# Two expert blocks before the overflow branch instead of one, and two buffers refilled in halves

## The reference

```
xs = h[row_tok]                      # tokens gathered by expert
def expert_block(xb, e):
    return (silu(xb @ w_gate[e]) * (xb @ w_up[e])) @ w_down[e]
y = zeros_like(h).at[row_tok].add(ys * row_w)   # each row scaled and added to its token
```

## Time and the profile before

| what | value |
|---|---|
| median of three runs | 1744.58 us |
| profiled execution | 1743.2 us, span 1741.4 us |
| TensorE matmul busy | 1624.5 us (93%) |
| VectorE busy | 653.8 us (38%) |
| read from HBM | 524.44 MB |
| mean granted TensorE clock | 0.973 |

### The profile page before, as it was taken

The page is one execution under the profiler, slowest core; times in us unless marked ns, Lnnn a source line. Parts: engine busy times, 40 slices in busy tenths (PEclk is TensorE's granted clock), DMA queues, the critical chain, the costliest instruction groups (busy, mean ns, idle before and its releaser), DMA issues.

```text
span 1741.4 us, 17712 instructions
## 1 busy us (share of the span) xinstructions
PE 1624.5 (93%) x6682; PEld 700.8 (40%) x6682; DVE 653.8 (38%) x1382; ACT 373.2 (21%) x919; POOL 71.2 (4%) x91
## 2 busy tenths in 40 slices
PE   5989998988999997998899999998889999979996
PEld 2435454462343332332344455444453333323332
DVE  2676665351323322323476122224531322322331
ACT  3023444231001010010410334333320101001000
POOL 1100000100000000000000000001000000000000
PEclk9999999999999998999999999998999999989999
DMA  9983823179999999999977021033389999999997
GB/s 353 372 308 100 288 97 146 52 285 389 430 426 426 425 428 427 427 428 419 364 240 243 1 97 49 1 124 123 141 365 420 427 423 427 429 426 426 428 427 293
DMA packets 109478, 526.64 MB, mean 302 GB/s; under 512 B 7921, under 2 KB 49122, under 8 KB 84682
## 3 DMA queue, kind: packets, MB, share of 16 engines
q1 hardware_dynamic: 80080, 486.56, 68.7%
q10 hardware_dynamic: 21322, 19.63, 3.6%
q0 software_dynamic: 7984, 19.22, 3.0%
HBM read 524.44 MB, written 8.48 MB: 306 GB/s over the span
## 4 chain that ended last, share of the span: by engine, by line
PE 81%; DMA 9%; DVE 5%; issue 2%; ACT 1%; SPq 1%; ACTq 0%; DVEq 0%
PE psum L2259 20%; PE psum L2290 11%; PE psum L2305 10%; PE psum L2016 10%; PE psum L1816 7%; PE psum L1988 4%; PE psum L1871 3%; DMA XN<-in_moe_w_up_dram 3%; DMA ring<-in_moe_w_up_dram 3%; DMA HT<-in_moe_w_down_dram 2%; PE psum L2237 2%; DVE W L1154 2%; DMA ring<-in_ada_w_dram 1%; PE psum L2123 1%; PE psum L1999 1%
## 5 line engine op out<-in xcount | busy, mean ns | idle before, releaser
L2259 PE MATMUL psum<-ring,V 128*32 128x512 f32 (+2 forms) x1376 | 352.3, 617 | 17.3 <-issue 9.4
L2305 PE MATMUL psum<-V,W 128*128 128x512 f32 x448 | 218.6, 613 | 3.6 <-DVE X L1606 1.1
L1606 DVE TENSOR_TENSOR X<-X,psum 128x512 f32<-128x512 f32 x224 | 153.7, 687 | 109.4 <-PE psum L2305 109.0
L2259 PEld LDWEIGHTS psum<-ring,V 128*32 128x32 f32 (+2 forms) x1376 | 115.9, 134 | 192.9 <-issue 192.6
L2290 PE MATMUL psum<-ring,V 128*64 128x512 f32 (+2 forms) x608 | 181.0, 596 | 0.8 <-issue 0.8
L1154 DVE SCALAR_TENSOR_TENSOR W<-ring,cact,W 128x512 f32<-128x512 f32 (+1 forms) x224 | 138.4, 618 | 7.7
L1046 ACT ACTIVATE V<-psum,modall,scls 128x128 f32<-128x128 f32 x216 | 81.2, 456 | 272.5 <-PE psum L2237 255.6
L2305 PEld LDWEIGHTS psum<-V,W 128*128 128x128 f32 x448 | 72.4, 188 | 148.5 <-DVE X L1606 85.3
L1055 ACT ACTIVATE V<-psum 128x512 f32<-128x512 f32 x28 | 16.7, 597 | 510.3 <-PE psum L2268 399.2
L2259 PE MATMUL psum<-HT,V 128*64 128x512 f32 (+2 forms) x224 | 102.4, 611 | 17.9 <-DMA XN<-in_moe_w_up_dram 17.5
L1816 PE MATMUL psum<-HT,ring 128*128 128x512 f32 x256 | 116.8, 602 | 0.0
(11 more groups left out here) (334 smaller groups left out, 1836.6 us busy)
## 6 DMA issues: line engine op xcount, KB each, us to landing
ring<-in_moe_w_up_dram SPq DMA_DIRECT2D x45, 2048.0 KB, 25.6
ring<-in_moe_w_gate_dram SPq DMA_DIRECT2D x41, 2048.0 KB, 25.3
ring<-in_moe_w_down_dram SPq DMA_DIRECT2D x38, 2048.0 KB, 25.4
ring<-in_ada_w_dram SPq DMA_DIRECT2D x16, 2048.0 KB, 15.8
HT<-in_moe_w_gate_dram SPq DMA_DIRECT2D x10, 2048.0 KB, 23.8
XN<-in_moe_w_up_dram SPq DMA_DIRECT2D x8, 2048.0 KB, 23.8
ring<-in_ada_w_dram ACTq DMA_DIRECT2D x16, 1024.0 KB, 5.2
T<-in_moe_w_up_dram SPq DMA_DIRECT2D x7, 2048.0 KB, 27.4
```

What stands on the lines that cost most here:

```text
L1606: return dve.tensor_tensor(x3[:, c, cols], x3[:, c, cols], sum_bank(p, hf, c), ALU.add)
L2259: ins = pe.matmul(bank[2 + 2 * i + b][half * w:(half + 1) * w, :], V[:, col:col + w], slot3(x)[:, k, :], start=(k == 0), stop=(k == KC - 1))
L2305: pe.matmul(sum_bank(p, hf, c), PICK[p % 2][:, c * P:(c + 1) * P], Y[:, hf * HALF:(hf + 1) * HALF], start=True, stop=True).then_inc(s["sum ...
```

## The change

It has two parts. First, `gate_up(1)` is taken out of `further_blocks()` and stands before the wait on `flag_ready`, the load of the flag and the branch. The order of TensorE's matmuls stays as it was. Second, loads 9 and 10, the first two that reuse a buffer (those of block 0's gates), are issued as two DMAs of 1 MB each. The first halves go out when TensorE has done four of the eight k-steps of block 0's gates (`first_gates`), since those four have used the first half of each buffer; the second halves go out when the gates are done, at which point load 9 went out before.

```diff
-DMAS = [2 if kind == "kq" else 1 for kind, _, _ in ORDER]
+REFILL = (len(HOMES[0]), len(HOMES[0]) + 1)
+DMAS = [2 if kind == "kq" or kind == "moe" and i in REFILL else 1 for kind, _, i in ORDER]
...
+        first_gates = sem("first_gates")
...
-                expert, ranked = {}, False
+                expert, ranked, refill = {}, False, {}
...
+                    if i in REFILL:
+                        sp.wait_ge(first_gates, l + 1)
+                        src = {"g": g, "u": u}[kind]
+                        sp.dma_start(slot(m + i)[:, 0:2 * D], src[:, 0:2 * D]).then_inc(w_in[SLOT[m + i]], 16)
+                        refill[i] = src
+                        if i == REFILL[1]:
+                            for x in REFILL:
+                                slot_free(m + x)
+                                sp.dma_start(slot(m + x)[:, 2 * D:4 * D], refill[x][:, 2 * D:4 * D]).then_inc(w_in[SLOT[m + x]], 16)
+                        continue
...
+                            if p == 0 and i == 0 and k == 3:
+                                ins.then_inc(first_gates, 1)
...
                 down(0)
 
+                gate_up(1)
+
                 def further_blocks():
 
-                    gate_up(1)
                     token_sums(0)
```

## The result

The changed kernel takes 1752.96 us, the median of five runs (1751.62 to 1753.43), against 1744.58 before (five runs, 1741.25 to 1746.43). The ratio is 1.005, with a 95% interval of 1.0039 to 1.0061: slower by 8.7 us, between 6.8 and 10.6. I had forecast 1750.6 in a range from 1740 to 1757. The profiled execution took 1752.78 us and its span is 1751.0, so 9.6 us more than before is to be found in it.

A forecast was written before the change was run, and what follows sets the result against it. TensorE and DMA are both near their limits; TensorE's lateness at block 5 less the slack delays each layer. +1.7 and +4.3 us make +6.0 on 1743.2, so 1749.2, plus 1.4 for the median: 1750.6, range 1740 to 1757.

The forecast's parts named there:

- the sum: Both layers' token-sum lateness, clock included, less slack: +1.7 us in layer 0, +4.3 in layer 1, together +6.0.
- the stall: TensorE idle at the moved branch, between block 1's ups and block 0's token sums: 5.9 us, bounds 4.5 and 7.4.
- the clock's cost: Half clock after idle time: 1.7 us at block 1's ups, 1.0 at the token sums, bounds 0 and 2.3 each.
- the gain of the refill: Loads 9 and 10 in halves put 2 MB in the queue earlier: 0.8 us in layer 0, 1.2 in layer 1.
- The slack: How late load 38 can go out at block 5 before the DMA stream breaks: 2.8 us, layer 1 3.0.
- The time behind the flag load: From TensorE's load of the flag to the first matmul behind the branch: 7.4 and 7.1 us.
- the cover: Matmuls queued ahead of the moved branch: about twelve of 0.11 us, hiding 1.3 us of its price.
- The lead of the stream: Transfers ahead before block 5, from refill and gate buffers freed sooner: 3.3 and 2.0 us.
- do not cancel: Rival that stall removed and stall added cancel, clock holding: total -1.7 us, 1742.9; chance 0.28.
- did not stay behind: Rival that the stall stays before block 1's gates and the moved branch is nearly free: -5.3 us, 1739.3; chance 0.07.
- the bounds: Rival with stall 7.4 us, clock 2.3 twice, refill gaining nothing: total +15, 1759.6; chance 0.10.

The follow-up runs named there:

- changed, again: The changed kernel, nothing altered, run once more for its profile; 1753.29 us.
- e1_branch_only: The changed kernel with loads 9 and 10 whole as before, only the branch moved behind block 1's ups; 1755.31 us, ratio 1.0058 to the kernel before.
- e2_refill_only: The changed kernel with the branch back in its old place, only the refill in halves kept; 1743.86 us, ratio 0.9999 to the kernel before.
- e3_branch_between: The changed kernel with the branch between block 1's gates and its ups, refill in halves; 1743.53 us, ratio 0.9991 to the kernel before.
- e4_no_branch: The changed kernel without TensorE's wait on the flag, its load and its branch; 1744.06 us, ratio 0.9997 to the kernel before.
- e5_delay3: The kernel before with three extra matmuls ahead of each layer's first token sums, no branch moved; 1748.50 us, ratio 1.0026 to the kernel before.
- e6_delay7: The kernel before with seven extra matmuls ahead of each layer's first token sums, no branch moved; 1755.13 us, ratio 1.0063 to the kernel before.
- e7_warm: The changed kernel with five extra matmuls between block 1's gates and ups, under the wait for load 13; 1749.02 us, ratio 1.0030 to the kernel before.
- e9_block9: The changed kernel with flag wait, flag load and branch moved between block 9's gates and ups; 1742.45 us, ratio 0.9993 to the kernel before.
- e10_block9_warm: e9_block9 plus five extra matmuls under the wait for load 13; 1743.44 us, ratio 0.9990 to the kernel before.
- e11_between_whole: e3_branch_between with loads 9 and 10 whole instead of in halves; 1744.01 us, ratio 0.9990 to the kernel before.

## Why the prediction was right

The mechanism was the one described, and the sum was 2.7 us too small (6.0 against 8.7). That it came so near is in part luck: the stall was shorter and the clock's cost a little larger than charged, the gain of the refill was missing in layer 0, and a term at the end of the program was not in the sum at all. Of the 9.6 us of the first profile only 4.2 lie in the two expert parts, of the 10.1 us of the second 8.7. The table gives, for both layers as layer 0 / layer 1, what each profiled execution has more than the one before, counted from block 0's gates: the issue of load 38, its landing, and the landing of the last down matrix (451.97 / 450.29 us before, from 391.51 to 843.48 and from 1276.69 to 1726.98).

| run | load 38 out | load 38 lands | last down lands |
|---|---|---|---|
| changed | 4.7 / 4.9 | 2.4 / 2.4 | 1.8 / 2.3 |
| changed, again | 7.7 / 6.1 | 5.5 / 3.7 | 4.9 / 3.8 |
| e1_branch_only | 4.0 / 8.5 | 1.8 / 6.1 | 1.1 / 6.0 |
| e2_refill_only | -0.1 / -1.2 | -0.3 / 0.4 | -0.4 / 0.6 |
| e3_branch_between | 0.0 / 2.1 | not recorded / -0.8 | -2.1 / -0.8 |
| e4_no_branch | -1.2 / -0.7 | -1.2 / -0.3 | -1.6 / -0.1 |
| e5_delay3 | 4.0 / 3.8 | 1.2 / 1.3 | 0.8 / 1.4 |
| e6_delay7 | 9.8 / 5.2 | 7.0 / 2.1 | 6.5 / 2.1 |
| e7_warm | 3.6 / 5.4 | 1.3 / 2.9 | 0.7 / 3.0 |
| e9_block9 | -1.8 / -0.8 | -2.0 / -0.3 | -2.4 / -0.3 |
| e10_block9_warm | -2.4 / -2.8 | not recorded / -1.5 | -2.3 / -1.6 |
| e11_between_whole | 0.8 / 1.6 | 0.4 / 0.0 | -0.7 / -0.4 |

*The slack.* In the six executions with a late TensorE, twelve cases, the first column less the second is 2.2 to 3.1 us, whether load 38 is 4 or 10 us late. (The lateness of load 38 stands here for that of TensorE, whose gates free its buffer.) I had taken 2.8 and 3.0; 2.3 and 2.5 hold for the changed kernel, as a lone load took 7.9 and 8.0 us and not 7.5. In layer 1 of e3_branch_between slack and lead together cover a lateness whole: load 38 goes out 2.1 us later than before and still lands sooner. The Trainium skill's fixed cost and rate (DMA: Bandwidth & Descriptors) gave an estimate of 6.8 us, and the traces do not agree: 7.4 to 8.1. That section is on DMAs that GpSimd issues, and these loads are SyncE's. In these twelve cases what is late at the landing of load 38 is late at the end of the part within 0.7 us. That the stream sets the time behind block 5, and TensorE up to it, is shown.

*The stall.* I had 5.9 us; it is 4.56 and 4.14. The time behind the flag load was right (7.3 and 6.9). The step that failed is the cover: "about twelve" matmuls queued ahead, 1.3 us. The ups end at 440.60 and 1327.98, 2.7 and 2.8 us behind the flag loads, which is some 24 matmul instructions of 0.11 us. What stayed nearly the same was the time that is covered, 2.5 us in the kernel before, and not the count. The stall moved with the branch in every run that shows it, and left with it. The rule of the Trainium skill's page Runtime: NRT & Kernel Launch (instruction fetch mechanics), that a taken branch waits for a fetch, fits this; no run shows that the stall is a fetch.

*The clock.* At the ups I charged 1.7 and it is 1.4 and 1.5 (8.44 on the chain of layer 0, and 8.53, for 7.07). At the token sums I charged 1.0 and it is 1.6 and 1.4 (9.58 and 9.38 for 7.97). In layer 0 of the second execution it is 2.4 at the ups and at least 2.1 at the token sums. These terms vary from one execution to the next more than anything else in the sum.

*The lead of the stream.* I had the stream 3.3 and 2.0 us ahead before block 5. Load 37, the last one issued before block 5's gates are done, lands 2.1 and 0.7 us sooner than before in the first profile, and no sooner in the second. In layer 0 the refill gives nothing: load 13 lands 38.1 us behind block 0's gates, 37.4 before. In layer 1 it lands 2.2 us sooner there (37.2 against 39.4), though other executions with the halves have up to 38.7. I had priced the refill by a dip in the GB/s, but the queue was not dry when load 9 went out before: load 8 landed 1.9 us later in layer 0 and 0.6 in layer 1. Both refills are in at 20.3 us behind block 0's gates in the changed kernel and 20.2 before in layer 0, at 20.0 and 21.4 in layer 1. The lead before block 5 is lost at block 5 in any case, but where load 13 lands sets when the ups start, and so the lateness. Because that lead is smaller than I thought, the expert parts of e3, e4 and e9 gain 1.7 to 2.9 us together and not 5.

*The sum.* Predicted +1.7 and +4.3; the first profile shows +1.8 and +2.3, the second +4.9 and +3.8. In the first, the token sums start 3.2 us late in layer 0, for which I had 3.5, and that agreement is luck: load 13 landed 1.4 us later than I put it, and the stall was 1.3 us shorter. In layer 1 they start 3.5 us late and not 6.3, since the stall was 1.8 us shorter and load 13 landed 1.0 us sooner than I put it.

*What I had no step for.* Behind the last landing of layer 1 the changed kernel takes 16.2 us to the end in both its profiles, 14.4 before. The chain after, then before (L2359 and L2344 are the last down products, L2319 and L2305 the last token sums):

```profile
1734.79 3.06 PE psum L2359 x16
1737.85 7.60 PE psum L2319 x16
```

```profile
1727.02 1.11 PE psum L2344 x8
...
1729.12 7.12 PE psum L2305 x16
```

The clock was granted at half there. It was in e1, e3, e4, e6, e9 and e11 too (15.8 to 16.2 us), and not in e2, e5, e7 and e10 (14.4 to 14.8). As e6 has neither part of the change, the fall does not need it; it gives back 1 to 2 us of what e3, e4 and e9 gained. Whether chance or the order of waits at the end decides it is open. Of the rest of the 9.6 us in the first profile, 2.5 lie before block 0 and 1.1 between the expert parts; the second execution has neither, and has its 10.1 us as -0.5, 4.9, 0.1, 3.8 and 1.8.

The rivals fall. The two parts do not cancel: the clock fell at both waits, and the median lies 10 us above that rival's. In layer 1 it was nearer than I allowed, though, for its token sums were to start 3.3 us late and start 3.5 us late in the first profile (4.7 in the second). The stall did not stay behind, since the gap behind the flag load is 7.3 and 6.9 us and not under 2. And the bounds were not all reached: 8.7 us and not 15.

## What to carry to other kernels

When a fixed order of buffers feeds an engine that is nearly as busy as the transfers, find the place where all buffers belong to the work at hand. The lateness of the engine there, less the time for which the queue still has transfers, is what the whole stage is late; nothing done further ahead counts except through that number. The branch of this kernel costs a stall of 4.1 to 5.1 us at its place, so put one like it where its engine waits longer than that for something else. Under a wait it cost nothing that could be measured here; one step behind it, in front of a long busy stretch, it cost its stall and the clock's fall with it.

## What the runs showed that I had not expected

Five matmuls a layer that compute nothing, 4.3 us of added work under a wait, did not make the changed kernel slower but, by the ratios, 3.5 us faster. They kept the granted clock at 2.4 GHz through the ups, and it stayed low for longer at the token sums instead.

An added 2.6 us of matmuls delayed load 38 by 3.8 to 4.0 us, and an added 6.0 us delayed it by 9.8 us in one layer and 5.2 in the other. In layer 0 the stall in the middle of block 1's gates comes 21 matmul instructions behind the branch before, 15 with six instructions added further on (three matmuls) and 7 with fourteen added (seven matmuls). Its place moved by as many instructions as were added, and it grew from 0.73 to 1.59 and 3.98 us. The rows of e5_delay3:

```profile
421.58 3.63 PE psum L2259 x15
425.21 1.59 issue
```

The added matmuls stand behind the gates in the program, but also in the copy on the other side of the branch, which lies ahead of them. So the place seems to hang on where the code lies and not on what it does. Layer 1 does not follow this (none, 1.34 us, none), and what the stall waits for is open.

And the last products of the program ran at half clock in eight of thirteen profiled executions and at full clock in the others, 1 to 2 us with no cause in the code around them.
